# A chunked RWKV-7 recurrence on one core: three low-rank products put in one place, norm sums, W products, key work and state banks moved

## The reference

```python
w = -jax.nn.softplus(-(w0 + jnp.tanh(wd) @ w2)) - 0.5      # first low-rank product: decay
decay = jnp.exp(-jnp.exp(w))
a = jax.nn.sigmoid(a0 + ad @ a2)                            # second: rate
g = jax.nn.sigmoid(gd) @ g2                                 # third: output gate
kk = heads(k * k_k)
kk = kk / jnp.maximum(jnp.sqrt(jnp.sum(kk * kk, axis=-1, keepdims=True)), 1e-12)
k = k * (1.0 + (a - 1.0) * k_a)

def step(S, inp):
    r_t, w_t, k_t, v_t, kk_t, a_t = inp
    sa = jnp.einsum('bhij,bhj->bhi', S, -kk_t)
    S = (S * w_t[:, :, None, :] + sa[..., :, None] * (kk_t * a_t)[:, :, None, :]
         + v_t[..., :, None] * k_t[..., None, :])
    return S, jnp.einsum('bhij,bhj->bhi', S, r_t)
# then: y is normalised by head (mean and variance over 64), scaled, shifted, a bonus is added, times g
```

## Time and profile before

| | us |
|---|---|
| three runs | 858.75, 859.91, 860.78 (median 859.91) |
| the profiled execution, and its span | 860.23, 858.5 |
| TensorE busy | 803.3 (94%) |
| VectorE, ScalarE, GpSimd busy | 462.7, 236.4, 282.0 |
| share of PE in the chain that ended last | 77% |

### The profile page before, as it was taken

The page is one execution under the profiler, slowest core; times in us unless marked ns, Lnnn a source line. Parts: engine busy times, 40 slices in busy tenths (PEclk is TensorE's granted clock), DMA queues, the critical chain, the costliest instruction groups (busy, mean ns, idle before and its releaser), DMA issues.

```text
span 858.5 us, 16620 instructions
## 1 busy us (share of the span) xinstructions
PE 803.3 (94%) x6791; PEld 537.1 (63%) x6791; DVE 462.7 (54%) x1174; ACT 236.4 (28%) x565; POOL 282.0 (33%) x267
## 2 busy tenths in 40 slices
PE   8999999999999999788989999999899999999950
PEld 8557544444444445777776555555798888888830
DVE  3760468888742134778763344344645555454534
ACT  6220021111200031556442123122232323232214
POOL 5810000000299700654660000000235565543332
PEclk9999999999999999999999999999999999999985
DMA  9944433344201021200004741213889998888639
GB/s 317 325 102 135 147 122 123 122 160 155 78 25 50 24 74 43 109 4 3 5 4 169 310 185 49 98 50 144 303 303 306 307 284 277 276 256 267 194 68 378
DMA packets 79716, 136.30 MB, mean 159 GB/s; under 512 B 17213, under 2 KB 51226, under 8 KB 79642
## 3 DMA queue, kind: packets, MB, share of 16 engines
q1 hardware_dynamic: 69338, 118.44, 39.5%
q0 software_dynamic: 10304, 16.82, 8.1%
HBM read 124.18 MB, written 29.92 MB: 179 GB/s over the span
## 4 chain that ended last, share of the span: by engine, by line
PE 77%; DVE 11%; DMA 5%; issue 3%; ACT 2%; SPq 1%; POOL 1%; DVEq 0%; POOLq 0%; ACTq 0%
PE banks L791 72%; PE banks L1432 3%; DVE REG_Y L1792 3%; DMA REG_P<-in_w_ada 1%; DMA xn_d<-REG_P 1%; DVE REG_P L2393 1%; ACT REG_P L1480 1%; DMA REG_P<-y_d 1%; PE banks L1363 1%; ACT REG_W L1480 1%; DVE REG_W L1899 1%; DVE mx L1902 1%; DMA REG_Y<-xn_d,tbl 1%; DMA y_d<-REG_Y,idx 1%; DVE REG_W L1941 1%
## 5 line engine op out<-in xcount | busy, mean ns | idle before, releaser
L791 PE MATMUL banks<-REG_W 128*128 128x512 f32 (+2 forms) x832 | 273.0, 497 | 0.3 <-DVE REG_W L1832 0.3
L791 PEld LDWEIGHTS banks<-REG_W 128*128 128x128 f32 (+1 forms) x832 | 125.5, 181 | 133.2 <-issue 132.5
L791 PE MATMUL banks<-REG_W,REG_Y 128*128 128x512 f32 x256 | 118.3, 599 | 1.4 <-DVE REG_Y L2348 1.1
L1480 ACT ACTIVATE REG_P<-banks 128x256 f32<-128x256 f32 (+2 forms) x102 | 46.7, 480 | 145.6 <-PE banks L791 127.0
L791 PE MATMUL banks<-REG_P 64*64 64x64 f32 (+3 forms) x2496 | 74.5, 236 | 10.6 <-issue 6.1
L791 PEld LDWEIGHTS banks<-REG_P 64*64 64x64 f32 (+1 forms) x2496 | 63.3, 138 | 20.9 <-issue 12.0
L1480 ACT ACTIVATE REG_Y<-banks,mod,s 128x128 f32<-128x128 f32 x136 | 51.2, 457 | 88.7 <-PE banks L1432 88.7
L791 PEld LDWEIGHTS banks<-REG_W,REG_Y 128*128 128x128 f32 x256 | 45.6, 191 | 44.3 <-issue 44.2
L791 PEld LDWEIGHTS banks<-REG_Y,REG_P 128*128 128x128 f32 (+1 forms) x616 | 63.2, 181 | 6.5 <-issue 6.5
L791 PE MATMUL banks<-REG_Y,REG_P 128*128 128x128 f32 (+1 forms) x616 | 66.5, 276 | 0.0
L635 POOL TENSOR_TENSOR REG_P<-REG_P 128x1040 f32<-128x1040 f32 x2 | 4.8, 2386 | 175.8 <-DVE REG_P L1878 175.8
(11 more groups left out here) (297 smaller groups left out, 1105.6 us busy)
## 6 DMA issues: line engine op xcount, KB each, us to landing
REG_P<-in_w_ada SPq DMA_DIRECT2D x20, 1024.0 KB, 6.6
REG_W<-in_w_in SPq DMA_DIRECT2D x17, 512.0 KB
REG_P<-in_moe_w_gate SPq DMA_DIRECT2D x17, 512.0 KB, 8.6
REG_W<-in_moe_w_gate SPq DMA_DIRECT2D x16, 512.0 KB, 6.5
REG_W<-in_moe_w_up SPq DMA_DIRECT2D x16, 512.0 KB, 9.6
REG_W<-in_moe_w_down SPq DMA_DIRECT2D x16, 512.0 KB, 15.2
REG_P<-in_moe_w_up SPq DMA_DIRECT2D x14, 512.0 KB, 13.5
REG_P<-in_moe_w_down SPq DMA_DIRECT2D x12, 512.0 KB, 20.5
```

Of the source, the lines that this page charges most:

```text
L791: return pe.matmul(o_, l, r, start=start, stop=stop, skip_group_check=True)
L1480: return act.activation(o_, i_, f, **kw)
```

## The change

It changes the order of work in the turns of the recurrence, and some banks:

1. `loras(m + 1)` is called once, between the halves of level 1, and issues for each half of the channels decay, rate, gate (before: the decay and rate products ahead of level 1, the gate products between the halves of level 2). The calls ahead of the recurrence take the same new inner order. `out_gate` moves from level 3 to level 1 on ScalarE, the rate's `tanh` from level 1 to level 2.
2. The tail norm's sums move from level 1 to level 2, behind a wait for the copy of the gate; VectorE's `norm_scale` from level 1 to 2; GpSimd's `norm_power` from behind level 2's mask to behind level 3's.
3. The W products move from level 2 to level 3, and from bank 6 to bank 5.
4. The state's products go to banks 6 and 7. They wait for the front norm's reader and no more for `w_re`, which is now waited for after them. The turned `Bt`, `Kt`, `KR` and the centred `v` use banks 2 and 3, so that level 1 waits for `w_vt` and `w_tka`.
5. `keys` moves from level 4 to level 3, `keys_finished` behind `norm_turned` of the front norm.
6. The router's bias uses bank 2.

```diff
@@ GpSimd, turn
-                    if l == 2 and m > 0:
+                    if l == 3 and m > 0:
                         norm_power(tail_norm(m - 1))
@@ TensorE
-            def loras(m, part=None):
+            def loras(m):
...
+                elif m > 1:
+                    pe.wait_ge(s["w_S"], 4 * m - 4)
+                    pe.wait_ge(s["w_ak"], 2 * m)
+                pe.wait_ge(s["w_tanh"], m + 1)
                 for p in range(2):
                     at, wide = slice(p * W2, (p + 1) * W2), slice(p * P, (p + 1) * P)
+                    mm(PS[6][:, at], lor[0:32, wide], lt[0:32, :])
+                    last = mm(PS[7][:, at], lor[32:64, wide], pT[32:64, B_LORA, PAD + m * W2:PAD + (m + 1) * W2])
...
+                    if p == 0:
                         pe.wait_ge(s["w_sg"], m + 1)
+                    last = mm(PS[5][:, at], lor[64:128, wide], lt[64:128, :])
+                last.then_inc(s["w_lora"], 1)
@@ TensorE, turn
-                if tail and more:
-                    for part in range(2):
-                        loras(m + 1, part)
...
-                            wait("w_tka", 3, 2)
+                        if l == 1:
+                            wait("w_tka", 3, 3)
                             wait("w_vt", 1, 1)
                         parts(l, n, bl[:, l % 2], xx, "t1", "w_t1p")
-                        for i in range(4 * n, 4 * n + 4) if l == 2 else ():
+                        for i in range(4 * n, 4 * n + 4) if l == 3 else ():
...
                     if l == 1:
-                        wait("w_tka", 3, 3)
-                        if tail:
-                            wait("w_ak", 2, 2)
-                            turn_sums(tail_norm(m - 1), sqt, tail_squares(m - 1))
-                    if tail and more and l == 2:
-                        for part in range(2, 4):
-                            loras(m + 1, part)
+                        if tail and more:
+                            loras(m + 1)
+                    if tail and l == 2:
+                        wait("w_xta", 6, 1)
+                        pe.wait_ge(s["w_gg"], min(m + 2, TURNS))
+                        turn_sums(tail_norm(m - 1), sqt, tail_squares(m - 1))
                     if tail and l == 3:
-                        wait("w_w1", 1, 1)
                         pe.wait_ge(s["w_tha"], min(m + 2, TURNS))
                         turn_flip(tail_norm(m - 1))
...
                     if more and l == 4:
-                        wait("w_gg", 1, 2)
+                        wait("w_w1", 1, 1)
@@ TensorE, behind the levels
-                wait("w_re", 2, 2)
+                pe.wait_ge(s["w_nbu"], front_norm(m + 1) if more else tail_norm(m - 1))
                 for n in range(2):
...
-                            mm(PS[2 + c][hb(h), at:at + HD], bt[cr(c), i, :], uz[cr(c), i, 0, :],
+                            mm(PS[6 + c][hb(h), at:at + HD], bt[cr(c), i, :], uz[cr(c), i, 0, :],
...
                 wait("w_pre", 4, 4)
+                wait("w_re", 2, 2)
@@ ScalarE, turn
-                    if l == 1 and more:
+                    if l == 1 and tail and more:
+                        out_gate(m + 1)
+                    if l == 2 and more:
                         rates(m + 1, (1,))
-                    if l == 2:
+                    if l == 3:
                         wait("w_w1p", 1, 1)
...
-                    if l == 3 and tail and more:
-                        out_gate(m + 1)
@@ VectorE, turn
-                    if tail and l == 1:
+                    if tail and l == 2:
                         norm_scale(tail_norm(m - 1), 1.0 / HD, GN_EPS, ALU.mult, ALU.add)
...
-                    if more and l == 4:
+                    if more and l == 3:
                         wait("w_tok", 3, 3)
                         keys(m + 1)
-                        keys_finished(m + 1)
                 if more:
                     norm_turned(front_norm(m + 1))
+                    keys_finished(m + 1)
```

More of the change, by code:

```diff
@@ L1000, in loras @@
                     pe.wait_ge(s["w_gg"], 1)
[L1001 to L1005, removed]
+                elif m > 1:
+                    pe.wait_ge(s["w_S"], 4 * m - 4)
+                    pe.wait_ge(s["w_ak"], 2 * m)
+                pe.wait_ge(s["w_tanh"], m + 1)
                 for p in range(2):
                     at, wide = slice(p * W2, (p + 1) * W2), slice(p * P, (p + 1) * P)
[L1008 to L1016, removed]
+                    mm(PS[6][:, at], lor[0:32, wide], lt[0:32, :])
+                    last = mm(PS[7][:, at], lor[32:64, wide], pT[32:64, B_LORA, PAD + m * W2:PAD + (m + 1) * W2])
+                    if p == 1:
+                        last.then_inc(s["w_lwa"], 1)
+                    if p == 0:
                         pe.wait_ge(s["w_sg"], m + 1)
-                        last = mm(PS[5][:, at], lor[64:128, wide], lt[64:128, :])
-                        if p == 1:
-                            last.then_inc(s["w_lora"], 1)
+                    last = mm(PS[5][:, at], lor[64:128, wide], lt[64:128, :])
+                last.then_inc(s["w_lora"], 1)
             def norm_sums(k, squares, count):
@@ L1240, in turn @@
                         parts(l, n, xT, t1, "x", "w_x2p")
-                        if l == 1 and tail and n == 0:
+                        if l == 2 and tail and n == 0:
                             pe.wait_ge(s["w_nrm"], tail_norm(m - 1))
@@ L1685, in turn @@
                         at = (n * 2 + p) * HD
-                        last = fn(S[:, (4 * m + i + 1) % 5, p, :], PS[2 + c][:, at:at + HD], scale=pend[:, m % 2, p, i:i + 1])
+                        last = fn(S[:, (4 * m + i + 1) % 5, p, :], PS[6 + c][:, at:at + HD], scale=pend[:, m % 2, p, i:i + 1])
                     last.then_inc(s["w_S"], 1)
@@ L2047, in keys_finished @@
                 ch.wait()
-                ch.step(tt(zt(B_K, B_K + 2, m), zt(B_K, B_K + 2, m), Kt, ALU.mult))
+                ch.note(tt(zt(B_K, B_K + 2, m), zt(B_K, B_K + 2, m), Kt, ALU.mult))
             def normed_keys(m):
@@ L2055, in key_operands @@
                 dve.wait_ge(s["w_exp"], m + 1)
-                ch.step(stt(aa, aa, 1.0, kkr, ALU.add, ALU.mult))
+                ch.note(stt(aa, aa, 1.0, kkr, ALU.add, ALU.mult))
+                ch.wait()
                 ch.note(stt(Bt, aa, 0.5, iP, ALU.mult, ALU.mult))
```

32 lines of the change are left out of this document (14 added, 18 removed).

## The result

The changed kernel takes 865.99 us in the median of 9 executions (862.46 to 868.65), the kernel before 860.22 (858.75 to 862.55) beside it on the same chip: a ratio of 1.0061 [1.0045, 1.0077]. A repetition (the twelfth experiment) gives 866.21 against 859.76, 1.0074 [1.0058, 1.0090]. So it is slower, as forecast, but by 5.8 and 6.4 us and not by 2.3, outside the range. The profiled execution took 864.5 us (span 862.7), which is 4.3 above that of before.

What follows compares the result with a forecast made beforehand. TensorE, busy for 94% of the span, was taken to bound the kernel. The turns summed to +1.5 us, with +0.76 from the early low-rank calls +2.3: 862.5 us profiled, 862.2 us median, range 857.3 to 864.6.

Steps and rivals of the forecast that it cites:

- The low-rank calls: Ahead of the recurrence and in level 1: mixed order drains TensorE at each tile change, 2.5 us against 2.1 per call.
- The two early calls: Low-rank calls ahead of the recurrence, in a full TensorE: the new order adds 0.76 us together.
- The rival of products side by side: Low-rank calls: gate runs beside the decay and rate pair, 1.06 us a call; 856.4 us in all, chance 0.17.
- The power and mask 4: GpSimd, turn 1: power ends 1.5 us behind VectorE's scan, mask 4 at 386.6, so `turn_back` in level 4 comes +1.3.
- the block: VectorE's scan holds up GpSimd's power through their shared ports; bounds 0 to 1.2 us a turn, twice.
- State products: End of each turn: they start without waiting for `re_`, so TensorE gains 0.8 us a turn, partly passed on through VectorE.
- Turn 0: ... its W copy and keys are covered; 0, then -0.8: Turn 0: moved W copy and keys cost nothing, so no change until the state products win 0.8 us.
- I let the gap at 388.53 move with the work ahead of it: Level 4: TensorE's gap without a releaser shifts with preceding work; its vanishing would return up to 0.6 us a turn.
- the chain is worse: Rival: `keys` fights GpSimd or gaps open at the power's wait; +1 us turns 1, 2, +0.5 turn 3; 864.7, chance 0.08.

Runs made afterwards that it cites:

- e12: The changed kernel run again unaltered, for its scatter (the twelfth experiment); 866.21 us, 1.0074 to the kernel before.
- e1: The changed kernel with the old inner order of the low-rank calls, gate products behind the decay and rate products; 863.32 us, 1.0056.
- e5: e1 with the tail norm's sums, `norm_scale` and GpSimd's power also back in their old places; 860.15 us, 0.9995.
- e2: The changed kernel with all four GpSimd scalings of a turn behind the front norm's power; 865.35 us, 1.0075.
- e14: The changed kernel with two of GpSimd's four scalings ahead of mask 3, not one each ahead of masks 4 and 5; 865.11 us, 1.0061.
- e13: The changed kernel with VectorE copying the tail norm's values and no power taken in turns 1 to 3, so the output differs; 911.59 us.
- e3: The changed kernel with `keys` and `keys_finished` back together in level 4; 864.99 us, 1.0065.
- e9: e5 with `keys` and `keys_finished` also back in level 4; 859.08 us, 0.9993.
- e4: The kernel before with only the state bank moves (items 4 and 6 of the change); 857.7 us, 0.9993.
- e10: e4 with the turn's first low-rank products waiting for the last state copy and no longer for `vt_`; 855.74 us, 0.9956.
- e11: e10 with the tail norm's `turn_flip` moved between the two near products of level 3's second half; 856.10 us, 0.9963.
- e15: e14 with `keys` and `keys_finished` back in level 4; 866.53 us, 1.0075.
- e6: The changed kernel with three idle products added ahead of level 4's wait for its mask in turns 1 to 3; 863.02 us, 1.0039.
- e7: The kernel before with 88 one-column products added ahead of the recurrence; 895.77 us, 1.0417.

## Why the prediction was wrong in size

The direction was right, and so was most of the course that was described; four terms of the sum were not. Counted from one first product with `G` to the next, the prediction's own marks say -0.8 for turn 0, +1.2 for turn 1 (+0.4 at its end, from -0.8), +1.45 for turn 2 and -0.35 for turn 3, in sum +1.5. The repetition, which has full clock in turns 1 to 3, shows +0.35, +1.93, +1.61 and -0.33, in sum 3.56. So 1.15 of the 2.1 that are missing lie in turn 0, 0.7 in turn 1, 0.2 in turn 2 and nothing in turn 3.

**The low-rank calls: right.** 2.5 was forecast, 2.51 measured, and 2.12 with the old order (e1). The two early calls cost 0.79 for a forecast of 0.76. The rival of products side by side is refuted.

**The power and mask 4: right.** The power is blocked until 1.43 behind the scan's end (forecast 1.5) and takes 2.48. The wait for mask 4 is there, and putting the sums back takes 4.0 us off (e5 against e1). Forecast at `turn_back` of turn 1 was +2.1 from turn 0's first `G` (+1.3, from -0.8); measured is 20.53 for 18.27, +2.26. That without the block all of this would come back is not shown: e2 and e14 win at level 4 and lose it elsewhere, and e13 wins 1.7 in turns 1 and 2 and can't be read beyond.

**State products: the mechanism right, but the step "Turn 0: ... its W copy and keys are covered; 0, then -0.8" failed.** Behind level 4's gap the 0.8 was won (8.34 for 9.14 until `G`), and what stands ahead of it took it back (12.46 for 11.64). The W products were costed at nothing, for they would lie under GpSimd's wait. Turn 0 has no tail norm and no such wait: the front sums waited 0.30 for the copy, the gap grew by 0.27, and the rest is spread over what lies before. In these two traces that is 0.8 to 1.1 of what was missing. How much of it is the W products' is less sure than it looks. e1 has the same turn 0, waits the same 0.30 and takes 20.18, 0.6 less than before; its low clock lasts until 352.5, and no gap opens in level 4. Turn 0 took 20.2 to 21.4 us in e1, e2, e5 and e12, whose TensorE work in it is in the same order.

The -0.8 itself was short in turn 1: 3.33 for 3.90 is 0.57, since 0.24 us pass between two records of the block, the same kind of gap in small. In turns 2 and 3 it is 3.08 for 3.90, the forecast 0.8.

**"I let the gap at 388.53 move with the work ahead of it": failed.** It grew in turn 1 from 0.57 to 0.97. In turn 2, from record to record, it was 1.08 us before, 1.57 after and 1.30 in e12. With the 0.24 in the state block these 0.40 are most of the 0.7 that are missing in turn 1. The gap is a late arrival of instructions:

```profile
DMA  0000000005000000000000000000000000000000
...
q8 instruction: 1, 0.02, 1.5%
```

This is the DMA view of the kernel after, from 388 to 392 us in 40 slices. One packet of 16 KB, one for each 256 records by the count above, moves from 388.92 to 389.88, and TensorE goes on at 391.32. Where TensorE has run without a wait, the packet starts to move about a microsecond behind the 38th of the 256 records, takes 0.9 to 1.4, and TensorE resumes 1.2 to 1.5 behind its end (this of the traces with gaps of over 0.5 us). The 38th, because the wait for mask 4 stands just ahead of it in turn 2, and there the packet comes only 1.16 behind the end of the wait (421.15 for 419.99; in e12 423.17 for 422.02). So the records left, some 220, end in a gap where TensorE could run them in less than some 3.6 us (an estimate, the sum of the three). A wait inside them pays for the delay; a wait ahead of them, like the new one for mask 4, does not. The two key steps beside GpSimd (2.0 us longer together) cost nothing that shows: undoing them (e3, e9) moved nothing.

The rival "the chain is worse" had these two causes: `keys` did fight with GpSimd, and gaps did grow around the power's wait. But it put 1 us each on turns 1 and 2 and 0.5 on turn 3, and nothing on turn 0, and measured are 0.7, 0.2 and 0 with 1.15 in turn 0. That it comes near the result (864.7) is in part luck.

**The clock: not in the forecast at all.** TensorE after, turn 2, and the window's clock:

```profile
423.79 1.50 PE L791 MATMUL banks<-REG_P 64*64 64x64 f32 x54 [1.36 <-issue]
```

```profile
424.00:428.00 4.00, 3.92 (x118) 3.70 (x111) 2.79 (x6) 2.46 (x6) 2.43 (x2) 0.62 0.01 4
```

Before it fell to the lower of its two levels, TensorE had been idle for 0.91 us at mask 4 and for 1.36 us in the gap, within 5 us. Such stretches cost 1.1 us in turn 2 (33.64 for 32.52) and 3.2 at the output products (e14). The Trainium skill's "TensorE: Matmul & The Clock Gate", section "A second HAM failure mode: psum-queue depth-cycling", tells of a kernel in which short idle times between groups of products, if frequent, were enough to let the clock swing between its two levels; these rows agree with that. But e12 was idle in the same two places for 1.18 and 1.08 us and kept full clock, so such idle time alone does not bring it about. Low stretches are found in the traces of both kernels (before at 620 us), so they can add to the scatter of both. Between turn 0 and 600 us the traces of before, e4, e9, e10 and e11 have none, and those of the changed kernel, e3, e5, e13, e14 and e15 have one or two each, while e1, e2, e6 and e12 have none.

The account for the changed kernel: 2.3 forecast, 2.1 more in the order of the work (turns of e12: 3.56 for 1.5 forecast), and 1.4 to 2 that the medians lie above it. The cause of this last part stays open. Low clock in more of the executions would fit the counts above, but profiles show one execution at a time; it is argued, not shown.

## What to carry to other kernels

Before an operation is moved on a helper engine, look at what stands behind it in that queue and, of VectorE and GpSimd, what the other runs beside it: in these runs the collision did not vanish, it moved to the next pair (e2, e5), and what counted was whether TensorE waited behind it. A gap without a releaser at a constant distance in instructions was here the supply of instructions, and it grew where a wait stood ahead of a dense stretch rather than in it. And once a buffer is moved, read the waits that guarded its old content: the one left behind was worth another 1.5 us in the turns (e10 against e4).

## What the runs showed of the hardware that was not expected

- TensorE's instructions came in packets of 16 KB, one for each 256 records, and it stood for up to 1.5 us where a dense stretch ran ahead of the next packet (1.51 in e1, 0.97 in the changed kernel at the same place; e7 for the count).
- 88 one-column products of 128 rows took some 34 us, four records and about 0.39 us each, most of it at the low clock: no cheap filler (e7).
- A VectorE operation of 0.69 us took 1.55 to 1.66 beside GpSimd's scalings, one of 1.22 took 2.32, and GpSimd's power of 8 columns 2.48 for 1.64: either side of the pair can be the one that waits.
- Three idle products of 128 columns in a wait did not make the kernel slower: 1.0039 for 1.0061 and 1.0074 (e6).
